# Linear attention of two sequences: no state product at a sequence's first tile, no update and no turned keys at its last

## What is computed

```
def step(S, inp):
    qc, kc, vc, bc = inp
    qe = qc * jnp.exp(bc)
    ke = kc * jnp.exp(-bc)
    A = jnp.einsum('bthk,bshk->bhts', qe, ke)
    A = jnp.where(tri, A, 0.0)
    o = jnp.einsum('bhts,bshv->bthv', A, vc) + jnp.einsum('bthk,bhkv->bthv', qe, S)
    bl = bc[:, -1]
    S = jnp.exp(bl)[..., None] * S + jnp.einsum(
        'bshk,bshv->bhkv', kc * jnp.exp(bl[:, None] - bc), vc)
    return S, o
S0 = jnp.zeros((B_, H, Dk, Dv), jnp.float32)
```

## Time and profile before

| | us |
|---|---|
| median of 3 runs | 2603.51 (2603.21 to 2603.67) |
| the profiled execution, from first to last instruction | 2600.5 |
| TensorE busy | 2564.2 (99%) |
| DVE busy | 1540.7 (59%) |
| ACT busy | 1067.7 (41%) |
| POOL busy | 244.6 (9%) |
| state products (L1283), TensorE's records added up | 42.3 |
| updates (L1270) | 41.1 |
| turned keys (L1246, L1247) | 21.8 |

### The profile page before, as it was taken

How to read it: one execution, slowest core, us unless ns; L and a number is a source line. 1 busy time by engine, 2 the same in 40 slices (tenths; PEclk the granted TensorE clock), 3 DMA queues, 4 the chain that set the end, 5 groups by cost and what they waited for, 6 DMA issues and landing times.

```text
span 2600.5 us, 40166 instructions
## 1 busy us (share of the span) xinstructions
PE 2564.2 (99%) x15290; PEld 2323.3 (89%) x15290; DVE 1540.7 (59%) x2292; ACT 1067.7 (41%) x1739; POOL 244.6 (9%) x407
## 2 busy tenths in 40 slices
PE   7999999999999999999999999999999999999998
PEld 5888888888888898888888888899999999999887
DVE  5545554564454635447443353988878867677843
ACT  5554245442444424544353333633333433333721
POOL 3001000100001000010010011011111300000000
PEclk9999999999999999999999999999999999999999
DMA  3122121221213212122163233144444862542021
GB/s 116 33 26 66 52 74 25 34 74 36 74 27 41 74 41 62 38 28 74 45 248 107 97 115 113 51 165 135 139 130 145 290 213 97 166 146 82 25 73 57
DMA packets 201705, 236.42 MB, mean 91 GB/s; under 512 B 14928, under 2 KB 172176, under 8 KB 201520
## 3 DMA queue, kind: packets, MB, share of 16 engines
q0 software_dynamic: 34576, 138.78, 16.8%
q1 hardware_dynamic: 164864, 95.05, 13.0%
q10 hardware_dynamic: 2080, 0.14, 0.1%
HBM read 168.73 MB, written 65.02 MB: 90 GB/s over the span
## 4 chain that ended last, share of the span: by engine, by line
PE 92%; DVE 4%; issue 2%; ACT 1%; DMA 0%; POOL 0%; POOLq 0%; DVEq 0%; ACTq 0%; SPq 0%
PE banks L1086 18%; PE banks L1088 18%; PE banks L1087 18%; PE banks L1444 5%; PE banks L1445 5%; PE banks L1446 5%; PE banks L1373 4%; PE banks L1375 4%; PE banks L1374 4%; PE banks L1201 2%; PE banks L1182 1%; PE banks L1283 1%; PE banks L1270 1%; PE banks L1192 1%; PE banks L1244 1%
## 5 line engine op out<-in xcount | busy, mean ns | idle before, releaser
L1086 PE MATMUL banks<-act_hi,w_hi 128*128 128x512 f32 (+1 forms) x2400 | 894.8, 373 | 2.4 <-DVE w_lo L2056 1.3
L1088 PE MATMUL banks<-act_hi,w_lo 128*128 128x512 f32 (+1 forms) x2400 | 851.9, 355 | 0.0
L1087 PE MATMUL banks<-act_lo,w_hi 128*128 128x512 f32 (+1 forms) x2400 | 850.4, 354 | 0.0
L1088 PEld LDWEIGHTS banks<-act_hi,w_lo 128*128 128x128 f32 x2400 | 452.6, 189 | 65.4
L1086 PEld LDWEIGHTS banks<-act_hi,w_hi 128*128 128x128 f32 x2400 | 453.9, 189 | 60.3 <-DVE w_lo L2056 1.9
L1087 PEld LDWEIGHTS banks<-act_lo,w_hi 128*128 128x128 f32 x2400 | 454.7, 189 | 53.5
L1444 PE MATMUL banks<-op,ring 128*128 128x320 f32 x896 | 277.3, 309 | 2.6 <-issue 1.9
L1445 PE MATMUL banks<-op,ring 128*128 128x320 f32 x896 | 276.9, 309 | 0.0
L1446 PE MATMUL banks<-op,ring 128*128 128x320 f32 x896 | 276.9, 309 | 0.0
L1724 ACT ACTIVATE work<-banks 128x512 f32<-128x512 f32 (+4 forms) x228 | 113.9, 505 | 333.2 <-PE banks L1088 333.1
L2056 DVE TENSOR_TENSOR w_lo<-w_raw,w_hi 128x1024 fp32r<-128x1024 f32 x110 | 130.3, 1184 | 78.9 <-ACT w_hi L1528 75.8
(11 more groups left out here) (358 smaller groups left out, 4290.2 us busy)
## 6 DMA issues: line engine op xcount, KB each, us to landing
w_raw<-in_w_in_dram SPq DMA_DIRECT2D x76, 512.0 KB
operand_scratch<-work POOLq DMA_DIRECT2D x112, 320.0 KB, 2.7
op_f<-operand_scratch POOLq DMA_DIRECT2D x28, 1280.0 KB, 6.4
w_raw<-in_w_mlp_dram SPq DMA_DIRECT2D x48, 512.0 KB, 5.5
work<-gate_scratch POOLq DMA_DIRECT2D x16, 640.0 KB, 5.4
gate_scratch<-work POOLq DMA_DIRECT2D x15, 640.0 KB, 3.3
raw<-in_w_mlp_dram SPq DMA_DIRECT2D x16, 512.0 KB, 5.6
work<-weight_scratch POOLq DMA_DIRECT2D x12, 640.0 KB, 5.9
```

What stands on the lines that cost most here:

```text
L1086: nc.tensor.matmul(out, wh, rh, start=first and k == 0, stop=False, skip_group_check=True)
L1087: nc.tensor.matmul(out, wh, rl, start=False, stop=False, skip_group_check=True)
L1088: mm = nc.tensor.matmul(out, wl, rh, start=False, stop=k == kt - 1, skip_group_check=True)
```

## The change

It names the steps at which a direction begins and ends a sequence: BEGINS has steps 0 and 8 for the forward direction and 0 and 2 for the backward one, ENDS has 7 and 9 and 1 and 9. Where a direction begins, TensorE leaves out its state product, and DVE copies the update to the state instead of scaling the old state and adding. Where it ends, there is no turned key, no copy of it on ACT, no update and no new state; the memsets of the state go too, POOL's at the head's start with its waits, and DVE's. In step 9 both directions end, so ACT has no copy at all, and masked(9) waits for TensorE's scores themselves. Where a backward state product is missing there is no backward output: ACT has two copies fewer, and in steps 7 and 9 DVE copies the forward output where it added. The counts of the semaphores follow (states_to, outputs_to and their like). The same numbers are computed otherwise.

```diff
-        state_zero = sem("state_zero")
...
+        BEGINS = ((0, TS // P), (0, TP // P))
+        ENDS = ((TS // P - 1, NT - 1), (TP // P - 1, NT - 1))
+        def states_to(j):
+            return sum(i not in ENDS[d] for i in range(j) for d in range(2))
+        def state_at(d, j):
+            return states_to(j) + (1 if d and j not in ENDS[0] else 0)
+        def outputs_to(j):
+            return j + sum(i not in BEGINS[1] for i in range(j))
+        def output_at(d, j):
+            return outputs_to(j) + d
+        STATES, OUTPUTS = states_to(NT), outputs_to(NT)
...
-                pool.wait_ge(prt_read, 30 * h + 31)
-                pool.wait_ge(pv_done, 30 * h + 31)
-                pool.wait_ge(exp_done, 30 * h + 31)
-                pool.wait_ge(prt_done, 30 * h + 31)
-                pool.wait_ge(max_done, 30 * h + 31)
-                pool.sem_inc(pool_passed, 1)
-                nc.gpsimd.memset(state[:], 0.0).then_inc(state_zero, 1)
...
-                    nc.tensor.transpose(bank[3][:, 2 * P:3 * P], ar[:, 2, fw], ident[:])
-                    nc.tensor.transpose(bank[3][:, 3 * P:4 * P], ar[:, 5, bw], ident[:]).then_inc(pre_done, 1)
+                    if j not in ENDS[0]:
+                        mm = nc.tensor.transpose(bank[3][:, 2 * P:3 * P], ar[:, 2, fw], ident[:])
+                    if j not in ENDS[1]:
+                        mm = nc.tensor.transpose(bank[3][:, 3 * P:4 * P], ar[:, 5, bw], ident[:])
+                    mm.then_inc(pre_done, 1)
...
                     for d, tile in ((0, j), (1, jb)):
-                        nc.tensor.matmul(bank[4 + d][:, 0:DV], kdn[:, j % 2, d, :], keyvals[:, tile, :],
-                                         start=True, stop=True).then_inc(u_done, 1)
+                        if j not in ENDS[d]:
+                            nc.tensor.matmul(bank[4 + d][:, 0:DV], kdn[:, j % 2, d, :], keyvals[:, tile, :],
+                                             start=True, stop=True).then_inc(u_done, 1)
...
+                    if j in BEGINS[0]:
+                        mm.then_inc(o_done, 1)
                     for d, tile in ((0, j), (1, jb)):
-                        for v in range(2):
-                            mm = nc.tensor.matmul(bank[6 + d][:, v * P:v * P + P], state[:, d, j % 2, v * P:v * P + P],
-                                                  ar[:, 3 * d, tile * P:tile * P + P],
-                                                  start=d == 1 and v == 0, stop=v == 1, skip_group_check=True)
-                        mm.then_inc(o_done, 1)
+                        if j not in BEGINS[d]:
+                            for v in range(2):
+                                mm = nc.tensor.matmul(bank[6 + d][:, v * P:v * P + P], state[:, d, j % 2, v * P:v * P + P],
+                                                      ar[:, 3 * d, tile * P:tile * P + P],
+                                                      start=d == 1 and v == 0, stop=v == 1, skip_group_check=True)
+                            mm.then_inc(o_done, 1)
...
-                    A(kdn[:, j % 2, :, :], bank[3][:, 2 * P:4 * P].rearrange("p (d s) -> p d s", d=2), ACT.Copy
+                    d0, d1 = (1 if j in ENDS[0] else 0), (1 if j in ENDS[1] else 2)
+                    A(kdn[:, j % 2, d0:d1, :], bank[3][:, (2 + d0) * P:(2 + d1) * P].rearrange("p (d s) -> p d s", s=P), ACT.Copy
...
-                if 0 <= j < NT and at_ == 3 and j + 1 < NT:
+                if 0 <= j < NT and at_ == 3 and j + 2 < NT:
                     decayed(j + 1)
...
+                        if d and j in BEGINS[1]:
+                            continue
...
                 def masked(j):
-                    dve.wait_ge(kdn_ready, 10 * h + j + 2)
+                    if j < NT - 1:
+                        dve.wait_ge(kdn_ready, 9 * h + j + 2)
+                    else:
+                        dve.wait_ge(pre_done, 10 * h + j + 2)
...
+                            if j in ENDS[d]:
+                                continue
...
-                            if (d, j) in ((0, TS // P - 1), (1, TP // P - 1)):
-                                ins = v_.memset(after, 0.0)
+                            if j in BEGINS[d]:
+                                ins = v_.tensor_copy(after, bank[4 + d][:, 0:DV])
...
+                        if d == 0 and NT - 1 - j in BEGINS[1]:
+                            v_.tensor_copy(o, src).then_inc(go_added, 1)
+                        else:
+                            v_.tensor_tensor(o, src, o, ALU.add).then_inc(go_added, 1)
```

More of the change, by code:

```diff
@@ L1240, in prelude @@
                         pe.wait_ge(a_ready, 10 * h + j + 1)
-                        pe.wait_ge(kdn_ready, 10 * h + j + 1)
+                        pe.wait_ge(kdn_ready, 9 * h + j + 1)
                     fw, bw = slice(j * P, j * P + P), slice((NT - 1 - j) * P, (NT - j) * P)
                     for d in range(2):
-                        nc.tensor.matmul(bank[3][:, d * P:d * P + P], ar[:, 3 * d + 1, fw], ar[:, 3 * d, fw],
-                                         start=True, stop=True, skip_group_check=True)
-                    nc.tensor.transpose(bank[3][:, 2 * P:3 * P], ar[:, 2, fw], ident[:])
-                    nc.tensor.transpose(bank[3][:, 3 * P:4 * P], ar[:, 5, bw], ident[:]).then_inc(pre_done, 1)
+                        mm = nc.tensor.matmul(bank[3][:, d * P:d * P + P], ar[:, 3 * d + 1, fw], ar[:, 3 * d, fw],
+                                              start=True, stop=True, skip_group_check=True)
+                    if j not in ENDS[0]:
[3 more added lines that the diff above has]
+                    mm.then_inc(pre_done, 1)
                 if tick == T_OUT + 11:
                     pe.wait_ge(osq_sum, h + 2)
-                    pe.wait_ge(s_ready, 20 * h + 21)
+                    pe.wait_ge(s_ready, STATES * h + STATES + 1)
                     for c, (t0, tw) in enumerate(CHUNKS):
@@ L1278, in gla_steps @@
                     for v in range(2):
-                        nc.tensor.matmul(bank[6][:, v * P:v * P + P], keyvals[:, j, v * P:v * P + P],
-                                         amat[:, j % 2, :], start=v == 0, stop=False, skip_group_check=True)
-                    for d, tile in ((0, j), (1, jb)):
-                        for v in range(2):
-                            mm = nc.tensor.matmul(bank[6 + d][:, v * P:v * P + P], state[:, d, j % 2, v * P:v * P + P],
-                                                  ar[:, 3 * d, tile * P:tile * P + P],
-                                                  start=d == 1 and v == 0, stop=v == 1, skip_group_check=True)
-                        mm.then_inc(o_done, 1)
+                        mm = nc.tensor.matmul(bank[6][:, v * P:v * P + P], keyvals[:, j, v * P:v * P + P],
+                                              amat[:, j % 2, :], start=v == 0, stop=v == 1 and j in BEGINS[0],
+                                              skip_group_check=True)
+                    if j in BEGINS[0]:
+                        mm.then_inc(o_done, 1)
+                    for d, tile in ((0, j), (1, jb)):
+                        if j not in BEGINS[d]:
[4 more added lines that the diff above has]
+                            mm.then_inc(o_done, 1)
                 if at_ == 2 and j + 1 < NT:
@@ L2333, in gla_steps @@
                     for d, tile in ((0, j), (1, NT - 1 - j)):
[L2334 removed]
+                        dve.wait_ge(o_done, OUTPUTS * h + output_at(d, j) + 2)
                         if j == 5:
[L2336 removed]
+                            dve.wait_ge(go_copied, outputs_to(5) * (h + 1) + 1)
                         o = o_gla[:, :, tile * P:tile * P + P]
[L2338 to L2339 removed]
+                        src = bank[6 + d][:, 0:DV].rearrange("p (v t) -> p v t", v=2)
+                        if d == 0 and NT - 1 - j in BEGINS[1]:
+                            v_.tensor_copy(o, src).then_inc(go_added, 1)
+                        else:
+                            v_.tensor_tensor(o, src, o, ALU.add).then_inc(go_added, 1)
             start = own.base + own.n
```

26 lines of the change are left out of this document (10 added, 16 removed).

## The result

| us | before | after |
|---|---|---|
| median of 5 runs, side by side | 2603.51 (2601.95 to 2609.42) | 2586.47 (2585.18 to 2587.82) |
| ratio after to before | | 0.993 [0.992, 0.994] |
| profiled execution, its span | 2600.5 | 2586.2 |
| granted clock in it, mean | 0.999 | 0.998 |

The kernel is faster by 17.0 us of medians, 0.7%; the interval of the ratio is 15.6 to 20.8 us. The forecast was a gain of 15.6 us and a median of 2587.9 us. One run of the kernel before took 2609.42 us and weighs in the ratio: the means of the five runs differ by 17.9 us, without that run by 16.6 us.

What follows compares the result with a forecast made beforehand. TensorE's queue, without holes, was taken to bound the kernel; 3.89 us per head over four heads made 15.6 us, so 2603.5 - 15.6 = 2587.9 us. The range given was 2586.0 to 2591.4 us.

Steps and rivals of the forecast that it cites:

- the Sum: Whole kernel: 15.6 us off the 2600.5 us span and the 2603.5 us median, giving 2584.9 and 2587.9 us.
- of start and end: Outside the profiled span: 3.0 us more in the median of the runs, 2603.5 against 2600.5 us.
- The pieces that go: TensorE's queue, per head: updates 1.75, state products 1.70, turned keys 0.44 us; 3.89 us, bounds 3.45 to 3.97 us.
- my two readings: State product price at head 0's first step: 0.111 us over 12 records, 0.101 us over eight; middle 0.106 us taken.
- The lower bounds for updates and turned keys: TensorE, per head: at least 1.55 us for updates and 0.28 us for turned keys, if part of the cost stays.
- Rival 1: TensorE's float32 records cost by columns, 0.06 us at 128: gain only 8.6 us, 2594.9 us; chance 4%.
- Rival 2: Step 9's masked product waits for DVE, 0.873 us per head go back: gain 12.1 us, 2591.4 us; chance 6%.
- (a): Step 9, masked scores from DVE to TensorE: margin shrinks from 1.2 to some 0.8 us, no wait.
- (b): Sum of squares behind the last tile: ready before TensorE takes it, margin of 2.4 us stays.
- The other engines: DVE, ACT and POOL: their edits stand beside TensorE's work and cost or gain nothing; no DMA added or moved.
- Rival 4: TensorE's queue is not shortened by the change, leaving 2603.5 us; chance 2%.
- (c): Turn of the loop over heads: DVE's chain moves with TensorE, gives nothing back; idle 1.3 us allowed either side.

Runs made afterwards that it cites:

- the repeat: Changed kernel run once more without any edit, beside the kernel before: 2586.9 us, ratio 0.9936.
- the kernel before with moved blocks: Kernel before, with DVE's four 64x64 blocks of halves_r and slope copy moved behind the first split of low weights: 2600.09 us, 0.9991.
- ends: Against the kernel before, only updates and turned keys of the last tiles go; state products and memsets stay: 2595.99 us, 0.9973.
- begins: Against the kernel before, only the state products of the first tiles go; updates and turned keys stay: 2595.15 us, 0.997.
- held: Changed kernel with DVE's blocks of halves_r made three times over and POOL's L879 memset waiting for the head's first low weights: 2592.95 us, 0.9957.
- unheld: Changed kernel with DVE's blocks of halves_r three times over; POOL's wait, one count too low, held nothing: 2595.26 us, 0.9971.
- the blocks behind the first split: Changed kernel with DVE's four blocks of halves_r and slope copy moved behind the head's first split of low weights: 2584.01 us, 0.9925.

## Where the prediction was right, and where it failed

**What failed.** The mechanism was right, a queue of TensorE without holes from which pieces were taken; the step that failed is the Sum. It took off 15.6 us and let only two things move the result towards faster, the queue's own bound of 15.9 us and the 1.3 us of idle time at the turns, so that its fast end was 2586.0 us, and the ratio gives 2585.3 us. Two terms in it had the wrong size. The state products stood at 0.106 us each and measured 0.111 us, 0.3 us in all. The stages behind the last head stood at nothing and were 1.4 us shorter in the repeat (1302.7 against 1304.1 us), 1.1 us of it at two waits of TensorE whose cause stays open. The view of waits before had them next to the two rows, and the prediction passed over them; before, and in the repeat:

```profile
PE banks L1444 <- issue: 1.9, 2, 1.0
```
```profile
PE banks L1465 <- issue: 0.9, 2, 0.7
```

The turns, allowed for with 1.3 us, took back 0.3 us. With 0.2 us less in head 0 that makes 16.7 us between the profiles. What lies between this and the 18.2 us of the ratio shows in no trace; the run of 2609.42 us accounts for most of it. That the median of the five runs lies in the range is as much chance as that the ratio lies outside: the repeat gives 15.8 us by its median and 16.7 us by its ratio.

The prediction's 3.0 us "of start and end" are two things: each run listed takes 1.5 to 1.9 us more than its own span, and the rest is the distance from the profiled execution to the median. It stands on both sides of the sum and changes nothing.

**The pieces that go.** Right. TensorE's queue is shorter by 3.95 us per head where 3.89 was forecast, inside the bounds of 3.45 to 3.97 and the 3.4 to 4.4 us outside which I would have been wrong. The term that was mis-sized is the price of a state product: 0.111 us each where I took the middle, 0.106 us; 0.08 us per head, 0.3 us in all. The first of my two readings had been the right one. In these kernels a product that goes saves its full distance whether its group goes whole or in half: the whole pair of updates of step 9 saved 0.87 us, a half 0.43 us, and two turned keys 0.22 us, one 0.11 us. The lower bounds for updates and turned keys fell with that.

**Rival 1, priced by columns.** Fallen. A float32 record of 128 columns costs 0.111 us where the rival said 0.06, and the whole gain is 17 us, not 8.6. The Trainium skill's N / 2.4 + 2.5 ns (TensorE: Matmul & The Clock Gate, Back-to-back issue gap) is an isolated gap by its own words; the rows of the changed kernel disagree with it for float32, as those of before did.

**Rival 2 and (a), step 9.** As forecast: a margin of 0.85 us, 0.8 worked out, no idle time. **(b)**: 2.4 us, unchanged. **The other engines**: nothing, and for POOL's memset a run of its own says so. **Rival 4** fell with the counts.

**(c), the turn.** This I got half right. The chain does move with TensorE, and the sum of idle time is 1.3 us before and 1.6 us in the repeat. DVE's issue time does vary, as I had feared, but between profiles of what is in effect the same kernel (5.74 and 6.48 us above). But I allowed "the loss of the idle 1.3 us or as much more", and one turn of the profile after lost 3.1 us. What I didn't see is a second price at that place: the memset of L879 can fall on DVE's blocks (about 1 us), and behind such a stall TensorE's clock may be at 1.2 GHz for 3.4 us (1.7 us). A near miss stood in the trace of before to be read: at its second turn DVE's last block began 0.08 us ahead of the memset, and took 0.19 us.

```profile
682.97 0.19 DVE L2349 TENSOR_SCALAR halves_r<-ones_r 64x64 fp32r<-64x64 f32 x1
```
```profile
683.05 1.22 POOL L859 MEMSET work<- 128x1280 f32 x1 [2.09 <-DMA oa_scratch<-work]
```

The kernel before seems to have such executions too: of its 12 runs beside the repeat, 8 had a mean clock of 0.999 and spans of 2600.2 to 2602.0 us, 4 had 0.998 and 2602.4 to 2604.2 us. But in the two later comparisons only 1 of 28 runs had 0.998, and one at 0.999 had a span of 2605.1 us. That a lower clock or a longer span in a run means a long turn is inferred, since only one execution in each set of runs has a trace.

**The gain beyond 15.6 us.** Of the 16.7 us between undisturbed profiles, the four heads give 15.3 us (3.75 + 11.56; 0.3 us of the 15.8 us in the records went back as idle time at the turns, and of the 0.2 us missing in head 0 0.15 us already stands at 283 us, ahead of the first instruction that changed). The remaining 1.4 us lie behind the last head, where nothing was changed. There TensorE has two waits in the second product of the MLP that the view calls issue, since it finds nothing that TensorE waited for, 1.9 us before and 0.9 us in the repeat. One of the two in each, before and after:

```profile
2057.07 0.38 PE L1444 MATMUL banks<-op,ring 128*128 128x320 f32 x1 [1.03 <-issue]
```
```profile
2043.05 0.38 PE L1465 MATMUL banks<-op,ring 128*128 128x320 f32 x1 [0.62 <-issue]
```

I can tie them to no edit: 2.0 us for the kernel before with moved blocks, 1.9 us for ends and 0.9 us for begins; 2.4 us held and 0.4 us unheld for the two kernels with longer blocks, which differ in one constant of one POOL wait. So about 1 us of the gain is of this kind, and its cause stays open; with one trace of each program but the changed one (0.8 and 0.9 us) it isn't even shown whether it goes with the program or with the execution.

**The fastest kernel** here has the change and the blocks behind the first split: 2584.01 us, 0.9925 [0.9912, 0.9939].

## What to carry to other kernels

Where one engine's queue has no holes, a removed instruction is worth its full distance from start to start, and the two halves of such a change add up (3.7 to 3.9 us here, against 3.95); when two readings of a distance differ by a change of kind, take the one that has it on both sides of the comparison. At a place where that engine waits bare, add up every other engine's work that could fall there, not only the chain that is named, and move what the waiting engine doesn't need behind what it does. Do not read a difference of 1 or 2 us out of one profile in a kernel of 2600 us: a single turn was worth 3 us. And give the stages that a change doesn't touch a term of their own in the range: here they moved by up to 1.9 us from one profile to another.

## What the hardware showed that I had not expected

**DVE and POOL.** DVE's casts and tensor_scalar operations of 64x64 elements take 0.19 us alone. In the profiles eight of them at the turns lay under POOL's memset of 128x1280. They took 1.08 to 1.23 us, and each ended 0.04 to 0.08 us behind the memset's end. Seven had started 0.01 to 0.17 us behind its start and one 0.02 us ahead of it; those that had started 0.07 us or more ahead kept their 0.19 us. The subtraction for the low weights (TENSOR_TENSOR, two inputs) takes 1.22 to 1.23 us with the memset beside it (the repeat, third turn) and without. The Trainium skill (SBUF — State Buffer, Who interferes with whom) says that copy, cast and tensor_scalar can take a pair of ports that GpSimd shares, as an exclusive lock for a whole instruction, while a tensor_tensor collides only with a GpSimd operation that reads SBUF. The traces agree in both, with the numbers above.

**The clock.** TensorE, busy for 99% of the span, lost half its clock for 3.4 us at turns with idle times of 1.74, 1.75 and 1.90 us, and kept it at turns with 1.80 and 1.85 us; up to 1.06 us it kept it at every turn profiled here. With 2.5 to 2.9 us it fell at each of three turns, once for 6.8 us. The length of the idle time alone doesn't decide: between 2436 and 2454 us each of the twelve profiles has one wait of 1.71 to 1.76 us for ACT, and none lost the clock there. The profile after:

```profile
2440.10 0.50 PE L1099 MATMUL banks<-p_hi,w_hi 128*128 128x512 f32 x1 [1.74 <-ACT work L2026]
```
```profile
2440.10:2443.50 3.40, 3.40 (x18) 2.92 (x19) 3.37 (x3) 2.74 (x5) 0.00 (x0) 1.00 0.33 95
```

What does decide, no run here shows.

**The loop's turn on DVE.** 4.1 us and some 3 us of issue time stand in the chain at a turn, and the profile after has 4.09 and 2.82 us at its first turn and 4.07 and 3.31 us at its third. The Trainium skill (Runtime: NRT & Kernel Launch, Instruction fetch mechanics) says that a taken branch to a target outside the window already fetched makes the engine wait for it. That would fit a loop of this length, but no run here isolates it.
